# Nine modulation units summed on VectorE instead of TensorE, in a two-block network on one Trainium2 core

## The reference, cut to what matters

```python
for layer in range(DEPTH):                     # DEPTH = 2
    mod = jax.nn.silu(c) @ w_ada[layer] + b_ada[layer]
    sh1, sc1, g1, sh2, sc2, g2 = jnp.split(mod[:, None, :], 6, axis=-1)
    hcur = rms_norm(x, norm1_g[layer]) * (1 + sc1) + sh1
    ...   # layer 0: proj = hcur @ ev_w_in, dilated attention, spatial gating, @ ev_w_out
    ...   # layer 1: proj = hcur @ od_w_in, convolution, stick-breaking attention, @ od_w_out
    x = x + g1 * mix
    hcur = rms_norm(x, norm2_g[layer]) * (1 + sc2) + sh2
    x = x + g2 * hierarchical_moe(hcur, ...)   # 16 experts, top 2 of one group per token
x = rms_norm(x, final_norm_g)
# second block
mod = jax.nn.silu(c) @ w_c[l] + b_c[l]
shift, scl, gate = jnp.split(mod, 3, axis=-1)
h = rms_norm_2(x, g_pre[l]) * (1.0 + scl[:, None, :]) + shift[:, None, :]
proj = h @ w_in[l]                             # then recurrence, windowed attention, two gated outputs
```

## Time and profile before

| | us |
|---|---|
| median of 3 runs (lowest to highest) | 1266.63 (1265.09 to 1269.27) |
| the profiled execution's own time | 1266.25 |
| its span | 1264.5 |
| TensorE matmul busy | 1198.5 (95%) |
| TensorE weight load busy | 702.5 (56%) |
| VectorE busy | 361.2 (29%) |
| ScalarE busy | 295.0 (23%) |
| GpSimd busy | 83.8 (7%) |
| HBM read | 350.84 MB, 278 GB/s over the span |
| chain that ended last | PE 80%, DMA 13%, DVE 2%, ACT 2%, issue 2% |

### The profile page before, as it was taken

How to read it: one execution, slowest core, us unless ns; L and a number is a source line. 1 busy time by engine, 2 the same in 40 slices (tenths; PEclk the granted TensorE clock), 3 DMA queues, 4 the chain that set the end, 5 groups by cost and what they waited for, 6 DMA issues and landing times.

```text
span 1264.5 us, 17438 instructions
## 1 busy us (share of the span) xinstructions
PE 1198.5 (95%) x7154; PEld 702.5 (56%) x7155; DVE 361.2 (29%) x1017; ACT 295.0 (23%) x626; POOL 83.8 (7%) x141
## 2 busy tenths in 40 slices
PE   4799999999999999999889999999999999999997
PEld 1566644544444448764433444445878778767773
DVE  0202414322212123952521121114211344342212
ACT  2112433111000021063400000103002545542101
POOL 2000011000000001500000000000000313200000
PEclk8799999899999999999989999999999999999999
DMA  9997999999999999831889999999834433424000
GB/s 336 313 387 243 308 280 385 382 425 428 430 429 428 429 397 208 247 133 67 360 355 404 404 422 429 427 429 388 204 133 146 152 97 130 150 80 145 17 1 33
DMA packets 90371, 352.77 MB, mean 279 GB/s; under 512 B 5284, under 2 KB 7500, under 8 KB 78028
## 3 DMA queue, kind: packets, MB, share of 16 engines
q1 hardware_dynamic: 83160, 340.68, 71.6%
q0 software_dynamic: 5488, 8.12, 3.1%
q10 hardware_dynamic: 1668, 3.21, 0.7%
HBM read 350.84 MB, written 1.15 MB: 278 GB/s over the span
## 4 chain that ended last, share of the span: by engine, by line
PE 80%; DMA 13%; DVE 2%; ACT 2%; issue 2%; SPq 1%; ACTq 0%; DVEq 0%
PE bank L456 28%; PE bank L751 20%; PE bank L469 12%; DMA ring<-in_moe_w_up 10%; PE bank L723 3%; PE bank L492 3%; PE bank L772 3%; DMA ring<-in_ev_w_in 2%; PE bank L505 2%; PE bank L1016 1%; SPq L368 1%; PE bank L603 1%; PE bank L640 1%; PE bank L643 1%; PE bank L629 1%
## 5 line engine op out<-in xcount | busy, mean ns | idle before, releaser
L456 PE MATMUL bank<-arena,ring 128*128 128x256 f32 x1600 | 356.0, 384 | 6.1 <-DVE arena L1539 2.8
L751 PE MATMUL bank<-ring,arena 128*32 128x512 f32 x3072 | 339.5, 600 | 12.1 <-issue 7.1
L456 PEld LDWEIGHTS bank<-arena,ring 128*128 128x128 f32 x1600 | 305.7, 192 | 54.6 <-issue 7.1
L751 PEld LDWEIGHTS bank<-ring,arena 128*32 128x32 f32 x3072 | 102.0, 111 | 237.0 <-issue 234.3
L469 PE MATMUL bank<-ring,arena 128*128 128x512 f32 x352 | 153.7, 594 | 2.3 <-DVE arena L2378 1.5
L469 PEld LDWEIGHTS bank<-ring,arena 128*128 128x128 f32 x352 | 66.2, 190 | 83.0 <-issue 79.6
L492 PE MATMUL bank<-ring,c_rep 128*32 128x512 f32 x480 | 64.3, 667 | 11.8 <-DMA ring<-in_w_ada 10.1
L2003 DVE TENSOR_TENSOR arena<-arena,bank 128x512 f32<-128x512 f32 x16 | 11.0, 688 | 203.8 <-PE bank L751 203.8
L723 PEld LDWEIGHTS bank<-arena 128*128 128x128 f32 x512 | 60.3, 197 | 13.6 <-issue 13.3
L723 PE MATMUL bank<-arena 128*128 128x128 f32 x512 | 63.4, 284 | 1.6 <-DVE arena L1971 1.5
L1283 ACT ACTIVATE arena<-bank 128x512 f32<-128x512 f32 x16 | 9.6, 597 | 216.8 <-PE bank L751 216.8
(11 more groups left out here) (300 smaller groups left out, 926.5 us busy)
## 6 DMA issues: line engine op xcount, KB each, us to landing
ring<-in_moe_w_gate SPq DMA_DIRECT2D x32, 2048.0 KB, 14.0
ring<-in_moe_w_up SPq DMA_DIRECT2D x32, 2048.0 KB, 16.7
ring<-in_moe_w_down SPq DMA_DIRECT2D x32, 2048.0 KB, 13.8
ring<-in_w_ada SPq DMA_DIRECT2D x24, 2048.0 KB, 14.1
ring<-in_w_in SPq DMA_DIRECT2D x16, 2048.0 KB, 8.9
ring<-in_w_c SPq DMA_DIRECT2D x6, 2048.0 KB, 9.2
ring<-in_ev_w_in SPq DMA_DIRECT2D x5, 2048.0 KB, 20.2
ring<-in_od_w_in SPq DMA_DIRECT2D x5, 2048.0 KB, 19.6
```

Of the source, the lines that this page charges most:

```text
L456: mm = pe.matmul(ps[k0][:, t * S:(t + 1) * S], w[:, k, c:c + P], rhs[:, k, :], start=(k == 0), stop=(k == KT - 1))
L751: mm = pe.matmul(bank[col:col + CHUNK, :], lhs[:, k, col:col + CHUNK], ring[:, s0 + e, cut], start=start, stop=stop, tile_position=(0, col))
```

## The change

The kernel gets a second way to multiply a modulation unit, on VectorE: `modulate(n)` multiplies the first of the unit's eight [128, 512] blocks by its column of silu(c) and adds the other seven with one `scalar_tensor_tensor` each, which leaves a [128, 512] part in SBUF. TensorE keeps only the columns of such a unit (`summed_columns`), and VectorE adds the bias for several units at once (`summed_cols`). Nine units go this way: `ada4` to `ada10` and `ada28`, `ada29`. A slot of the ring that held such a unit is freed by VectorE's sum (`modulation_summed`), which `read_wait` tells SP, and counts of `unit_done` are worked out without these units (`done_at`, `copied_at`).

The places move too. `ada4` to `ada7` are summed between the projections and `ada8` to `ada10` after the scores of head 1; their columns stand in the middle of `ev2`, after it, and between the two halves of `ev3`. Head 0 has no unit, heads 1 to 7 have one each (`ada11` to `ada17`). The routing of layer 0 has five units instead of six (two mains and two columns before the ranks, one main and two columns after), that of layer 1 four (one main and two columns before, one main and one column after). `ada28` and `ada29` are loaded and summed in the second block's projections, their columns stand after `in4`, and `half_gate` is computed after them.

```diff
 def stream():
     u = [("ada", n) for n in range(4)]
-    u += [("ev", 0), ("ada", 4), ("ev", 1), ("ada", 5), ("ev", 2)]
-    u += [("ev", 4), ("ada", 6), ("ev", 3), ("ada", 7)]
-    u += [("ada", n) for n in range(8, 17)]
+    u += [("ev", 0), ("ada", 4), ("ev", 1), ("ada", 5), ("ada", 6), ("ev", 2), ("ada", 7)]
+    u += [("ev", 4), ("ada", 8), ("ev", 3), ("ada", 9)]
+    u += [("ada", n) for n in range(10, 18)]
     u += [("evo", 0), ("evo", 1)]
-    u += [("ada", n) for n in range(17, 23)]
+    u += [("ada", n) for n in range(18, 23)]
...
-    u += [("ada", n) for n in range(24, 30)]
+    u += [("ada", n) for n in range(24, 28)]
     u += [("moe", 1)] * (6 * PAIRS)
-    u += [("in", n) for n in (0, 1, 4, 6, 8, 2, 3, 10, 11, 12, 13, 5, 7, 9, 14, 15)]
+    u += [("in", 0), ("in", 1), ("ada", 28), ("ada", 29)]
+    u += [("in", n) for n in (4, 6, 8, 2, 3, 10, 11, 12, 13, 5, 7, 9, 14, 15)]
...
+SUMMED = tuple(range(4, 11)) + (28, 29)
...
+        def read_wait(eng, n):
+            if summed_unit(units[n]):
+                eng.wait_ge(sem("modulation_summed"), summed_at(n))
+            else:
+                eng.wait_ge(unit_done, done_at(n))
...
-        ROUTE_UNITS = ((17, 6), (24, 6))
+        ROUTE_UNITS = ((18, 5), (24, 4))
...
-        ROUTE_SOON = 3
+        ROUTE_SOON = (4, 3)
...
# SyncE, fetch
-                    sp.wait_ge(unit_done, n - RING + 1)
+                    read_wait(sp, n - RING)
...
# TensorE
+            def summed_columns(lo, hi, base=None):
+                base = lo if base is None else base
+                if lo == base:
+                    pe.wait_ge(sem("ada_ready"), lo)
+                for n in range(lo, hi):
+                    pe.wait_ge(sem("modulation_summed"), summed_at(unit_of[f"ada{n}"]))
+                    part = sum_of(n)
+                    for c in range(4):
+                        o = 4 * (n - base) + c
+                        mm = pe.matmul(ps[4][:, o:o + 1], part[:, c * P:(c + 1) * P], ones[:, 0:1],
+                                       start=True, stop=True)
+                    mm.then_inc(sem("ada_cols_full"), 1)
+                ada[1] = hi
...
-                for n in range(ROUTE_SOON):
+                for n in range(2):
                     ada_columns()
...
                 ada_main()
+                for n in range(2, ROUTE_SOON[layer]):
+                    ada_columns()
                 pe.wait_ge(sem("over_ready"), layer + 1)
...
-                for n in range(units - ROUTE_SOON - 1):
-                    ada_columns()
...
-            ada_main()
             by_channel("ev1", hT)
-            ada_columns()
-            ada_main()
-            by_token("ev2", hT)
-            ada_columns()
+            by_token("ev2", hT, lambda: summed_columns(4, 6))
+            summed_columns(6, 8)
...
-                    by_channel("ev3", hT)
-                elif h > TWO_A:
-                    ada_columns()
+                    by_channel("ev3", hT, (0,))
+                    summed_columns(8, 11)
+                    by_channel("ev3", hT, (1,))
...
             by_channel("in4", hT)
+            summed_columns(28, 30)
...
# VectorE
+            def modulate(n):
+                at_ = unit_of[f"ada{n}"]
+                dve.wait_ge(loaded[at_ % RING], 16 * (at_ // RING + 1))
+                dve.wait_ge(sem("setup_ready"), 4 if n >= 2 * ADA_SEG else 1)
+                w, part = ring[:, at_ % RING, :].rearrange("p (k c) -> p k c", c=512), sum_of(n)
+                for k in range(KT):
+                    scale = c_rep[:, n // (2 * ADA_SEG), k, 0:1]
+                    if k == 0:
+                        ins = dve.tensor_scalar(part, w[:, 0, :], scale, None, ALU.mult)
+                    else:
+                        step.wait()
+                        ins = stt(part, w[:, k, :], scale, part, ALU.mult, ALU.add)
+                    if k < KT - 1:
+                        step(ins)
+                ins.then_inc(sem("modulation_summed"), 1)
...
             take("ev0", 1, qT[:, 2:4, :], 0.125)
-            ada_cols()
+            for n in (4, 5, 6):
+                modulate(n)
             take("ev1", 1, kT[:, 2:4, :])
-            ada_cols()
+            modulate(7)
+            summed_cols(4, 6)
             take("ev2", 1, v_tok[:, 1, :])
...
                     score_probs("dilated")
+                if h == 0:
+                    for n in (8, 9, 10):
+                        modulate(n)
+                if h == 1:
+                    summed_cols(8, 11)
...
+            modulate(28)
+            modulate(29)
             dve.memset(xa_raw[:, :, 0:2], 0.0)
...
             pool.wait_ge(sem("ada_ready"), 6)
             broadcast_gate(0, mod[:, 16:24])
             affine_by_row(0)
+            pool.wait_ge(sem("ada_ready"), 11)
```

More of the change, by code:

```diff
@@ L191, in program @@
         neg_ge, neg_ones = at(82, P), at(82.5, P)
-        route_part = [at(32 + 2 * n, HW) for n in range(6)]
+        route_part = [at(32 + 2 * n, HW) for n in range(5)]
         gate_diag, logit_parts = at(44, D), at(48, S)
@@ L427, in weights @@
             def weights():
+                while summed_unit(units[unit[0]]):
+                    unit[0] += 1
                 n = unit[0]
```

94 lines of the change are left out of this document (56 added, 38 removed).

## The result

The changed kernel takes 1273.98 us (median of 9 runs, 1272.12 to 1278.65), the kernel before 1268.63 in the same comparison (9 runs, 1263.53 to 1271.98): ratio 1.004, 95% interval 1.0023 to 1.0057. The forecast was 1260.1 and its range ended at 1268.5, so both missed, on the slow side. The profiled execution took 1273.09, its span is 1271.4 against 1264.5 before.

What follows compares the result with a forecast made beforehand. TensorE was taken as the bound (95% busy), with loads beside it in layer 0's experts. Terms of -8.5 up to those experts' end and +2.4 behind gave -6.1 from 1266.25, so 1260.1 us; range 1252 to 1268.5.

Steps and rivals of the forecast that it cites:

- two stops by `issue` in layer 1's loop: Layer 1 stops of 4.08 and 2.97 us; matmuls behind them lost 3.1 and 1.8, used to price evo0's low clock.
- A sum on VectorE, 5.6 us a unit: VectorE's sum of one modulation unit: 0.70 us a step with its handover, 5.6 us a unit.
- VectorE the bound: Rival: steps take the long form's 1.24 us, a unit 10 us, projections wait for VectorE; about 1273, chance 0.08.
- The 2 us of room: At ev3, sums of ada8 to ada10 end by 118.5 to 120.5; TensorE needs the last at 122.5.
- a sign that the prediction had named for being wrong: VectorE ending a wait of over 1 us in the projections would show the prediction wrong.
- Projections and heads, evo0 reached at 166.9: Up to evo0: projections and heads 0 and 1 save 0.7, heads 5 to 7 10.2; TensorE arrives at 166.9, not 177.84.
- Stop before evo0, 4.6, start 171.5; clock 2.5: evo0's unit lands at 171.4, TensorE waits 4.6 us, starts at 171.5; the lowered clock then costs 2.5, leaving -3.8.
- the first chance of 0.14: First rival, evo0 without a stop; counted among the outcomes faster by over 0.3%, chance 0.14.
- Routing of layer 0, -4.3: Layer 0's routing: gather comes 2.3 us earlier and at full clock takes another 2.0 less, in all -4.3.
- Experts, -8.5: Layer 0's experts end 8.5 us earlier, limited by the loads; bounds 8.1 and 10.4.
- Two trailing columns, nothing: The two columns behind layer 0's experts (1.84 us) save nothing, since VectorE's tile is ready when they end.
- Layer 1 and after, +2.4: Layer 1 and second block: gather +1.7 (half clock), experts' loads -1.3, columns of ada28 and ada29 +2.0; in all +2.4.

Runs made afterwards that it cites:

- experiment 2: Changed kernel plus never-executed matmuls ahead of each expert loop's end (57 in layer 0, 23 in layer 1), placing code as in the kernel before: 1259.43 us, ratio 0.9936.
- experiment 12: On top of experiment 2, the gain of the affine rows (POOL's short pieces) computed beside head 1 instead of head 4: 1257.0 us, ratio 0.991.
- experiments 12 and 13: Experiment 12, then on top of it the columns of ada8 to ada10 moved behind both halves of ev3: 1257.0 us and 1256.26 us.
- experiment 9: Changed kernel with code placed as in the kernel before, without the branch hint behind the experts: 1263.82 us, ratio 0.9957.
- experiment 3: Kernel before with 7 never-executed matmuls ahead of the end of layer 0's expert loop, some 28 instructions on: 1267.07 us, ratio 0.9995.

## Why the prediction was wrong, and where it was right

**The step that failed is one that the sum did not have.** The forecast put the path from the last scatter to the next layer at nothing: instruction for instruction the same, less two columns that "save nothing". The shorter program moved the end of the loop and the target of the branch behind it against the blocks in which code is loaded, and that cost two stops of 5.43 and 4.54 us, each with a stretch of half clock (0.50 up to 476.0 and up to 889.0): 1274 with both, 1259.4, 1259.3 and 1261.4 in the three placements without. The forecast of 1260.1 is near the time of the change without them, in part by luck: it forecast a gain of 6.1 from one profiled execution at 1266.25, and experiment 2 gains 8.6 between the medians, from 1268.07. It was not among the rivals, and could have been: rows 12 have two stops by `issue` in layer 1's loop, which I priced for their clock and did not ask the cause of.

Term by term:

- *A sum on VectorE, 5.6 us a unit*: 5.9, 0.752 a step instead of 0.70. Nearer the 0.684 of the short form than the 1.24 of the long, as argued. The rival "VectorE the bound" did not occur in the changed kernel's profile; its price of 1273 is close to the result by chance alone. The 2 us of room were not there: in eight of the twelve other profiles of the changed program TensorE waited 2.2 to 4.5 us for the last sum, a sign that the prediction had named for being wrong. The sums are no slower there. VectorE waits for the load of `ada9`'s unit, 3.4 us already in the changed kernel's own profile and 6.2 in experiment 12, and the last sum ends at 124.2 and not by 120.5; in the changed kernel's own profile the half clock in `ev3` hides it.
- *Projections and heads, evo0 reached at 166.9*: 168.05 (171.71 less 3.66). The half clock fell once more than forecast, in the first half of `ev3` (8.9 us for 7.1; 0.50 from 114.2 to 117.6).
- *Stop before evo0, 4.6, start 171.5; clock 2.5*: 3.66, 171.71, 1.7 (26.83 against 25.14; 0.50 from 172.2 to 175.6). In all -4.4 for -3.8. The slow stretch of the stream is POOL's, as experiments 12 and 13 show, but without it the stop is still 1.76: the prediction laid the whole stop on it. The pieces are 64 on q0, 32 of 256 bytes and 32 of 4 (157.0 to 159.3 us before, 158.3 to 161.0 in the changed kernel), not of 4 bytes alone. An `evo0` without a stop, for which the first chance of 0.14 stands, no profile shows with TensorE in time: the shortest stop there is 0.82, in experiment 9.
- *Routing of layer 0, -4.3*: the gather starts 5.5 ahead where -6.1 was the running sum, the experts 7.5 ahead where 8.1 was. The full clock came as forecast (1.00 in 225:230, where before had 0.50).
- *Experts, -8.5*: -8.3. This fits better than it should: in the eleven profiles of the changed program whose code is alike up to there this scatter starts between 456.69 and 464.23, and `evo0` between 170.8 and 177.1, and the changed kernel's own is the earliest of them. The middle one, 460.7, is 4.3 ahead of the 465.01 of before, whose copy in experiment 3 starts at 468.2. So one profile is good to a few us here, and the match is luck in good part.
- *Two trailing columns, nothing*: right. From scatter to first transpose 5.26 us both times.
- *Layer 1 and after, +2.4*: wrong even without the stops. In experiment 2, where it can be read, this part gains 2.2: the gather lies as far behind `od0` as before (152.54, 152.62) and takes 3.82, not up to 2.0 longer, so +1.7 is -0.1; from the gather to the last scatter 238.64 us against 243.30, -4.7 where -1.3 stood (the loads no longer bind and one stop by `issue` is gone); the columns of `ada28` and `ada29` and what follows +2.5 where +2.0 stood. Why that stop is gone was not tried apart.

In the changed kernel none of layer 1's gain is seen. Its start is late, and the DMA stands nearly empty: the stretches in layer 1's first experts, where before had 421 and 200 GB/s:

```profile
630.00:640.00 10.00, 3.65 (x18) 1.52 (x21) 4.84 (x16) 2.07 (x4) 0.00 (x0) 0.82 0.33 131
640.00:650.00 10.00, 10.00 (x84) 3.24 (x80) 0.00 (x0) 0.60 (x1) 0.00 (x0) 0.84 0.11 25
```

The ring is full and waits for slots that only TensorE can free: SyncE waits 21.5 us there for a matmul of the experts. My account of what follows is argued, not shown: what is not loaded there is missing later, and the last scatter comes at 869.49, when before's did (869.42). Experiment 2 starts these experts 5.8 us earlier and ends them 9.1 us earlier. It has a gap as deep, 5 GB/s in 630:640, but a shorter one (364 GB/s in 640:650). What the longer gap alone costs was not tried apart.

## What to carry to other kernels

When an edit changes the length of a program that has loops and far branches, count where the loop's end and the branch's target fall in the blocks of instructions (256 to a piece of 16 KB here, by the counts above), and look at the instruction queue in the trace: here a 16 KB piece lay inside each stop by `issue` that a shift of the code removed, and a few dozen instructions of padding, or none, can be worth more than the edit. Judge an edit to such a kernel in two or three placements before its verdict is taken as its own. And ask of every `issue` in the rows what it waited for before its price is used for something else.

## What the runs showed that I had not expected

Code that never runs moved the time by 14.7 us, 1.2%, where nine matrix units taken from TensorE moved it by 9. A branch hint helps or does nothing depending on that placement (5.38 us in one layer, none in the other). And 64 short pieces of another queue (q0 in experiment 2, 32 of 256 bytes and 32 of 4, from 159.3 to 161.8 us) hold up the stream of 2 KB pieces from 387 down to 67 GB/s for 5 us, while the share of the DMA engines' time reads 2.20; yet the unit behind this stretch landed only 1.3 us earlier when it was gone.
